# Expert weights loaded as pairs of units, 128 rows of 8 KB, into six buffers, on a one-core Trainium2 decoder step

## The chip, the cores and the metric

The kernel is one program on one core of a Trainium2 chip. The metric is the device time of one execution in microseconds (us); the time of a kernel is the median over its runs. The profile is of one execution, and its span is counted from the first to the last instruction.

## The reference

The reference is one inference step of a 2-layer decoder for 264 tokens (256 of a prompt and 8 samples), d_model = 1024, all in float32. What the change touches is the expert layer at the end of layer 1:

```python
def _swiglu(h, wg, wu, wd):
    return (jax.nn.silu(h @ wg) * (h @ wu)) @ wd

def _moe(h, router, wg, wu, wd):
    logits = jnp.einsum('btd,de->bte', h.astype(jnp.float32), router.astype(jnp.float32))
    top_v, top_i = lax.top_k(logits, TOP_K)            # TOP_K = 2 of N_EXPERTS = 8
    probs = jax.nn.softmax(top_v, axis=-1)
    gates = jnp.sum(jax.nn.one_hot(top_i, N_EXPERTS, dtype=jnp.float32) * probs[..., None], axis=-2)
    y = jnp.zeros_like(h)
    for e in range(N_EXPERTS):                          # wg, wu: 1024 x 2816, wd: 2816 x 1024
        y = y + gates[..., e:e + 1].astype(h.dtype) * _swiglu(h, wg[e], wu[e], wd[e])
    return y
```

## The kernel before, in words

The program has four stages in a row: the mixer of layer 0, its dense FFN, the mixer of layer 1, and the experts. Each engine has its own instruction stream, and semaphores are all that orders one against another.

**Jobs and units.** The tokens that chose an expert are gathered in jobs of at most 96 rows (CAP). Each job is one pass of a loop (`Fori(0, n_jobs)`) on PE, ACT, DVE and SP, and reads all weights of its expert. The weights are cut on the host in 66 units (N_FFN) of 128 partitions x 4 KB, 512 KB each: units 0 to 43 hold gate and up columns (11 chunks of 256 columns, four units a chunk: gate with the first and the second half of the 1024 input features, then up with both), and units 44 to 65 hold 128 rows each of the down matrix. In DRAM the units of all experts lie behind one another, so a unit is 512 contiguous KB.

**The path of a unit.** SP loads it into one of 11 slots (RING_X): six of the tensor `ring`, four in `early`, one in `qkv`. ACT copies it, rounded to fp32r, to one of four buffers `w_hi` (L773). DVE subtracts that from the unit and writes the rest to `w_lo` (L1233), which bumps `lo_done`. PE then multiplies with it (L1286, function `split_products`: hi x hi, hi x lo, lo x hi), 12 matmuls of 256 columns in a gate or up unit and 6 of 512 columns in a down unit. ACT takes a `w_hi` buffer again once PE has used the unit four back.

**What SP waits for.** SP issues in order. In `load_units` (L429) the load of a unit waits until the low part of the unit that was last in its slot, 11 units back, is done. It doesn't wait for PE. After unit 43 of each job SP issues `load_rows`: the token rows of the next job (384 KB, L435) and 0.8 KB of gates and token numbers (L437).

**Around the chunks.** When the products of a chunk are complete, ACT makes silu of the gate part (L783), DVE multiplies it by the up part into `prod_job` (L1251), PE turns that in two transposes of 96 rows x 128 columns (L1632), ACT and DVE split the turned part (L788, L1255). These are the stationary side of the down products. Around unit 52 PE turns the next job's token rows (L1576) and ACT and DVE split them. In units 3 to 6 the output of the job before is spread to the tokens with 16 matmuls (L1586, L1587).

**Before job 0.** The normalized rows of the second layer are turned to token-major form: PE transposes (L1548), and ACT copies three groups of 128 x 1024 from PSUM to `h_tok` (L743; the profile calls it by its tensor, `gs`). From there POOL scatters the rows to `h_rows` in DRAM (L493), and PE gathers the rows of job 0 (L1566) when DVE has worked out the routing (the last of it `take`, L1184). The first six units are loaded as the slots come free in the mixer (L406), five more once the state outputs are stored (L422).

Of the kernel before, what the change touches and what calls it, by code (L numbers as in the profile page):

```python
# [24 lines left out]
ALU = mybir.AluOpType  # L25
ACT = mybir.ActivationFunctionType
# [4 lines left out]
P = 128  # L31
D = 1024
# [23 lines left out]
N_FFN = 66  # L56
N_LAYER = N_PROJ + N_MIX + N_WO
RING = 6
SPLIT = 4
LEAD = 3  # L60
CHUNK = 256
# [7 lines left out]
NEXT_H = 52  # L69
RING_X = 11  # L70
Y_AT = 3
# [7 lines left out]
def build(nc, a, o):  # L79

    ctx = ExitStack()
    with ctx:
# [3 lines left out]
        def sem(name):  # L86
            return ctx.enter_context(nc.semaphore(name))
# [135 lines left out]

        slot_loaded = [sem(f"slot_loaded{i}") for i in range(RING_X)]
        units_used = sem("units_used")
# [140 lines left out]
        def uses_before(position):  # L366

            return sum(1 for p in ordinal if p < position and p % RING == position % RING)


        n0 = [uses_before(first_position("experts") + s) for s in range(RING)] + [0] * (RING_X - RING)

        def slot_x(s):

            if s < RING:
                return ring[:, s, :, :].rearrange("p k n -> p (k n)")
            if s < RING + 4:
                return early[:, (s - RING) * D:(s - RING + 1) * D]
            return qkv[:, :, :].rearrange("p t n -> p (t n)")[:, 0:D]

# [15 lines left out]
        def _(sp):  # L396
# [18 lines left out]
            for i in range(N_LAYER):  # L415
                load_static("mix1", i, a["w_mixer"][1, PROJ[i] if i < N_PROJ else i])
            for i in range(RING):
                load_static("experts", i, a["w_exp"][i])
            sp.wait_ge(state_out, 16 * 4 * DEPTH)
            sp.wait_ge(units_used, base_ord["mix1"] + N_PROJ + N_MIX)  # L420
            for i in range(RING, RING_X):
                sp.dma_start(slot_x(i), a["w_exp"][i]).then_inc(slot_loaded[i], 16)  # L422

            def load_units(expert, job, r0, r1):
                with sp.Fori(r0, r1) as r:
                    for s in range(RING_X):

                        sp.wait_ge(lo_done, job * N_FFN + r * RING_X + (n_split + s + 1 - RING_X))
                        sp.dma_start(slot_x(s), a["w_exp"][bass.ds(expert * N_FFN + r * RING_X + s, 1), :, :].rearrange("a p n -> p (a n)")  # L429
                                     ).then_inc(slot_loaded[s], 16)  # L430

# [6 lines left out]

            late = N_FFN // RING_X * 2 // 3
            load_units(0, 0, 1, late)  # L440
            sp.wait_ge(rows_stored, 16 * 12)
            load_rows(0)
            load_units(0, 0, late, N_FFN // RING_X)
            sp.wait_ge(jobs_done, 1)
            n_jobs = sp.value_load(jobs[0:1, MAX_JOBS:MAX_JOBS + 1], min_val=2, max_val=MAX_JOBS)
            with sp.Fori(1, n_jobs) as job:
                expert = sp.value_load(jobs[0:1, bass.ds(job, 1)], min_val=0, max_val=NE - 1)
                load_units(expert, job, 0, late)
                load_rows(job)
                load_units(expert, job, late, N_FFN // RING_X)  # L450

# [54 lines left out]
        def _(act):  # L506
# [38 lines left out]
            for l in range(DEPTH):  # L545
# [193 lines left out]
                else:  # L739

                    for m in range(3):
                        act.wait_ge(h_tr, m + 1)
                        A(h_tok[:, m, :], psum[:, (0, 2, 6)[m]:(0, 2, 6)[m] + 2, :].rearrange("p b n -> p (b n)"), ACT.Copy).then_inc(h_tok_done, 1)  # L743
                    act.wait_ge(gates_exp_in, 1)
# [17 lines left out]
                    with act.Fori(0, n_jobs) as job:  # L762
                        for u in range(N_FFN):

                            if u == Y_AT:

                                y_high(job)
                            act.wait_ge(slot_loaded[u % RING_X], job * (16 * N_FFN // RING_X) + 16 * (n0[u % RING_X] + u // RING_X + 1))
                            if buffer_x(u) == Y_AT % SPLIT and u < Y_AT + SPLIT:
                                act.wait_ge(scatter_mm, job * KD + KD)  # L770
                            else:
                                act.wait_ge(units_used, job * N_FFN + (base_ord["experts"] + used_before_x(u) + 1))
                            A(w_hi[:, buffer_x(u), :], slot_x(u % RING_X), ACT.Copy).then_inc(hi_done, 1)  # L773
                            if u == NEXT_H + 1:
# [23 lines left out]
        def _(dve):  # L798
# [50 lines left out]
            for l in range(DEPTH):  # L849
# [278 lines left out]
                else:  # L1128
# [101 lines left out]
                    with dve.Fori(0, n_jobs) as job:  # L1230
                        for u in range(N_FFN):
                            dve.wait_ge(hi_done, job * N_FFN + (n_split + u + 1))
                            V.tensor_tensor(w_lo[:, buffer_x(u), :], slot_x(u % RING_X), w_hi[:, buffer_x(u), :], ALU.subtract).then_inc(lo_done, 1)  # L1233
                            if u == Y_AT - 1:
# [32 lines left out]
        def _(pe):  # L1267
# [40 lines left out]
            for l in range(DEPTH):  # L1308
# [228 lines left out]
                else:  # L1537
# [56 lines left out]
                    with pe.Fori(0, n_jobs) as job:  # L1594
                        for u in range(N_FFN):
# [28 lines left out]
                            if u % 4 == 3 and 0 <= ch < NCH:  # L1624

                                pe.wait_ge(chunk_done, job * NCH + (ch + 1))
                                if ch >= 2:
                                    pe.wait_ge(act_lo_done, job * NCH + (ch - 1))
                                elif ch == 0:
                                    pe.wait_ge(down_taken, job * KD + 2 * KD)  # L1630
                                for i in range(2):
                                    last = nc.tensor.transpose(psum[:, 4 + ch % 2, i * CAP:(i + 1) * CAP], prod_job[:, ch % 2, i * P:(i + 1) * P], ident[0:CAP, 0:CAP])  # L1632
                                last.then_inc(act_tr, 1)
# [132 lines left out]
```

## Time and profile before

| | |
|---|---|
| median of 3 runs | 1713.52 us (1711.02 to 1717.63) |
| the profiled execution | 1717.27 us, span 1715.5 us |
| expert stage | from about 872 us of the span to its end, 8 jobs |
| loads of the queue q1 | 103888 packets, 375.15 MB |
| mean granted TensorE clock | 0.965 |

In the rows below, a busy time is that of an engine in us, PE is the matrix engine, PEld its weight loads, DVE the vector engine, ACT the scalar engine, SPq the DMA queue's issuing engine. The durations of matmuls overlap, as the engine is pipelined; their pace is read from their starts.

### The profile page before, as it was taken

What the parts mean: (1) busy time and instruction counts of PE and PEld (TensorE: products, weight loads), DVE (VectorE), ACT (ScalarE), POOL (GpSimd) and SP (SyncE); (2) the same over time, 40 slices, a digit from 0 to 9 for tenths busy, and PEclk for the clock granted to TensorE, in tenths of its full rate; (3) what the DMA queues carried; (4) which work ended last, traced back from release to release, by engine and by line L of the source; (5) the groups of instructions that cost most, each with busy time, mean ns of one, the idle gap of its engine ahead of it and who ended that gap; (6) DMA issues with size and microseconds to landing.
All of it is one profiled execution on the core that took longest, in us unless ns stands there. A gap on an engine that the chain in (4) does not pass through costs nothing.

```text
span 1715.5 us, 30826 instructions
## 1 busy us (share of the span) xinstructions
PE 1596.8 (93%) x10899; PEld 1436.0 (84%) x10899; DVE 1215.6 (71%) x1740; ACT 941.4 (55%) x1299; POOL 34.5 (2%) x53
## 2 busy tenths in 40 slices
PE   6998999899998998999879999999999999999995
PEld 4988977899986988977779797897979889797984
DVE  4777755544203776855369898898989889898984
ACT  4632242444103642242258787777877778787773
POOL 0000002000000000000030000000000000000000
PEclk9999799999999999899789999999999999999997
DMA  6542135855444541124369999998998999899990
GB/s 250 183 92 62 38 92 176 304 180 181 129 149 153 200 116 50 50 88 164 135 215 362 352 335 348 339 372 302 370 352 330 347 341 368 310 359 356 331 353 32
DMA packets 108453, 397.39 MB, mean 232 GB/s; under 512 B 13553, under 2 KB 13600, under 8 KB 107616
## 3 DMA queue, kind: packets, MB, share of 16 engines
q1 hardware_dynamic: 103888, 375.15, 61.8%
q0 software_dynamic: 4496, 21.28, 3.5%
q8 instruction: 48, 0.79, 0.2%
q14 instruction: 21, 0.17, 0.0%
HBM read 380.94 MB, written 16.43 MB: 232 GB/s over the span
## 4 chain that ended last, share of the span: by engine, by line
PE 83%; DVE 10%; ACT 4%; issue 2%; DMA 1%; SPq 0%; DVEq 0%; ACTq 0%; POOL 0%
PE psum L1286 57%; PE psum L1532 5%; PE psum L1319 3%; PE psum L1497 2%; PE psum L1499 2%; DVE w_lo L815 1%; PE psum L1392 1%; PE psum L1456 1%; PE psum L1399 1%; DVE w_lo L1233 1%; DVE qkv L885 1%; ACT w_hi L773 1%; PE psum L1403 1%; ACT w_hi L536 1%; DVE c L916 1%
## 5 line engine op out<-in xcount | busy, mean ns | idle before, releaser
L1286 PE MATMUL psum<-w_hi,h_hi 128*96 128x256 f32 x1408 | 402.0, 286 | 22.5 <-DVE w_lo L1233 22.5
L1286 PE MATMUL psum<-w_hi,h_lo 128*96 128x256 f32 x1408 | 395.2, 281 | 0.0
L1286 PE MATMUL psum<-w_lo,h_hi 128*96 128x256 f32 x1408 | 394.5, 280 | 0.0
L1233 DVE TENSOR_TENSOR w_lo<-ring,w_hi 128x1024 fp32r<-128x1024 f32 x288 | 343.3, 1221 | 33.8 <-ACT w_hi L773 33.7
L773 ACT ACTIVATE w_hi<-ring 128x1024 fp32r<-128x1024 f32 x288 | 301.9, 1058 | 28.1 <-PE psum L1286 16.9
L1286 PE MATMUL psum<-hid_hi,w_hi 128*128 128x264 f32 x992 | 290.2, 293 | 8.1 <-DVE hid_lo L821 6.1
L1286 PE MATMUL psum<-hid_lo,w_hi 128*128 128x264 f32 x992 | 285.3, 288 | 0.0
L1286 PE MATMUL psum<-hid_hi,w_lo 128*128 128x264 f32 x992 | 285.0, 287 | 0.0
L1233 DVE TENSOR_TENSOR w_lo<-early,w_hi 128x1024 fp32r<-128x1024 f32 x192 | 231.0, 1222 | 36.0 <-ACT w_hi L773 36.0
L1286 PEld LDWEIGHTS psum<-w_hi,h_hi 128*96 128x96 f32 x1408 | 228.8, 162 | 27.1 <-DVE w_lo L1233 26.4
L1286 PEld LDWEIGHTS psum<-w_hi,h_lo 128*96 128x96 f32 x1408 | 229.0, 163 | 0.0
L1286 PEld LDWEIGHTS psum<-w_lo,h_hi 128*96 128x96 f32 x1408 | 228.4, 162 | 0.3
L773 ACT ACTIVATE w_hi<-early 128x1024 fp32r<-128x1024 f32 x192 | 201.4, 1057 | 41.1 <-PE psum L1587 19.6
L815 DVE TENSOR_TENSOR w_lo<-ring,w_hi 128x1024 fp32r<-128x1024 f32 x124 | 150.4, 1220 | 81.4 <-ACT w_hi L536 81.3
L536 ACT ACTIVATE w_hi<-ring 128x1024 fp32r<-128x1024 f32 x124 | 130.7, 1058 | 136.3 <-PE psum L1286 94.7
L1286 PEld LDWEIGHTS psum<-hid_hi,w_hi 128*128 128x128 f32 x992 | 191.0, 193 | 12.9 <-issue 8.1
L1286 PEld LDWEIGHTS psum<-hid_lo,w_hi 128*128 128x128 f32 x992 | 191.4, 193 | 0.1
L1286 PEld LDWEIGHTS psum<-hid_hi,w_lo 128*128 128x128 f32 x992 | 190.3, 192 | 0.0
L1286 PE MATMUL psum<-w_hi,hid_hi 128*96 128x512 f32 x352 | 140.6, 399 | 11.5 <-DVE w_lo L1233 11.5
L1286 PE MATMUL psum<-w_hi,hid_lo 128*96 128x512 f32 x352 | 138.3, 393 | 0.0
L1286 PE MATMUL psum<-w_lo,hid_hi 128*96 128x512 f32 x352 | 137.9, 392 | 0.0
L916 DVE SCALAR_TENSOR_TENSOR c<-u_pad,prm,c 128x256 f32<-128x256 f32 x240 | 97.0, 477 | 0.0
(301 smaller groups left out, 1962.1 us busy)
## 6 DMA issues: line engine op xcount, KB each, us to landing
ring<-in_w_exp SPq DMA_DIRECT2D x288, 512.0 KB, 5.4
early<-in_w_exp SPq DMA_DIRECT2D x192, 512.0 KB, 5.4
ring<-in_w_mixer SPq DMA_DIRECT2D x112, 512.0 KB, 3.5
ring<-in_w_ffn SPq DMA_DIRECT2D x66, 512.0 KB, 3.5
qkv<-in_w_exp SPq DMA_DIRECT2D x48, 512.0 KB, 5.6
h_rows<-work POOLq DMA_DIRECT2D x12, 480.0 KB, 14.1
early<-in_s POOLq DMA_DIRECT2D x2, 2048.0 KB, 8.5
out_ss<-early POOLq DMA_DIRECT2D x2, 2048.0 KB, 9.1
```

Of the source, the lines that this page charges most:

```text
L536: A(w_hi[:, n % SPLIT, :], ring[:, p % RING, :, :].rearrange("p k n -> p (k n)"), ACT.Copy).then_inc(hi_done, 1)
L773: A(w_hi[:, buffer_x(u), :], slot_x(u % RING_X), ACT.Copy).then_inc(hi_done, 1)
L815: V.tensor_tensor(w_lo[:, n % SPLIT, :], ring[:, p % RING, :, :].rearrange("p k n -> p (k n)"), w_hi[:, n % SPLIT, :], ALU.subtract).then_ ...
L885: ins = V.scalar_tensor_tensor(qkv[:, t, 0:TP], q_pad[:, t, tap:tap + TP], w, qkv[:, t, 0:TP], ALU.mult, ALU.add)
L916: ins = V.scalar_tensor_tensor(c[:, j, 0:TP], u_pad[:, j, tap:tap + TP], w, c[:, j, 0:TP], ALU.mult, ALU.add)
L1233: V.tensor_tensor(w_lo[:, buffer_x(u), :], slot_x(u % RING_X), w_hi[:, buffer_x(u), :], ALU.subtract).then_inc(lo_done, 1)
L1286: last = M(out, lhs[x], rhs[w], start=(start and n == 0), stop=(stop and n == 2))
L1319: last = M(psum[:, i % 4, 0:T], w[:, k, :], hT[:, k, :], start=(k == 0), stop=(k == KD - 1))
L1392: last = M(pair(4)[:, u, :], units(7)[:, u, :], units(4)[:, u, :], start=True, stop=True)
L1497: M(psum[:, 2 * (t % 2), 0:T], w[:, j, :], c[:, j, :], start=(j == 0), stop=(j == CT - 1))
L1499: last = M(psum[:, 2 * (t % 2) + 1, 0:T], w[:, CT + h, :], qkv[:, 8 + h, :], start=(h == 0), stop=(h == H - 1))
L1532: last = M(psum[:, 6 + t % 2, 0:T], w[:, i % KD, :], act_all[:, f, :], start=(f == 0), stop=(f == FT - 1))
```

## The change

The same DRAM array is read as pairs: the 256 rows of two neighbouring units are taken two by two, so that partition p (of 128) gets rows 2p and 2p+1 of the pair, 8 contiguous KB. The first half of what a partition gets is "unit" 2g for the engines, the second half "unit" 2g+1. A unit now holds the even or the odd rows of the pair, so the other side of the products is put in the same order: `h_tok` is written by six copies of 128 x 512 whose innermost step is 512 elements, in place of three of 128 x 1024, and the transposes of `prod_job` read every second column. The host lays out nothing differently.

The 11 slots of 4 KB become six of 8 KB (three in `ring`, two in `early`, one in `qkv`). `SLOT_OF` gives the slot of each of the 33 pairs of a job: slots 0 to 5 three times over, then 0 to 4 three times over. A load waits until both units of the pair that was last in its slot have their low parts, six pairs back for pairs 5 to 22 and five back for the others, over the end of a job too. ACT waits for the load at each first unit of a pair. SP's loop over rounds of 11 units is written out as 33 loads.

```diff
--- before.py
+++ after.py
@@ -67,7 +67,8 @@
 JOB_ROWS = (MAX_JOBS + 1) * CAP
 ZERO_ROWS = 120
 NEXT_H = 52
-RING_X = 11
+PAIRS = N_FFN // 2
+SLOT_OF = list(range(6)) * 3 + list(range(5)) * 3
 Y_AT = 3
 
 
@@ -221,7 +222,8 @@
         jobs = ctx.enter_context(nc.sbuf_tensor("jobs", [P, MAX_JOBS + 1], mybir.dt.int32))
 
 
-        slot_loaded = [sem(f"slot_loaded{i}") for i in range(RING_X)]
+        slot_loaded = [sem(f"slot_loaded{i}") for i in range(RING)]
+        pair_loaded = [sem(f"pair_loaded{i}") for i in range(6)]
         units_used = sem("units_used")
         x_loaded = sem("x_loaded")
         consts_loaded = sem("consts_loaded")
@@ -368,15 +370,30 @@
             return sum(1 for p in ordinal if p < position and p % RING == position % RING)
 
 
-        n0 = [uses_before(first_position("experts") + s) for s in range(RING)] + [0] * (RING_X - RING)
-
-        def slot_x(s):
-
-            if s < RING:
-                return ring[:, s, :, :].rearrange("p k n -> p (k n)")
-            if s < RING + 4:
-                return early[:, (s - RING) * D:(s - RING + 1) * D]
-            return qkv[:, :, :].rearrange("p t n -> p (t n)")[:, 0:D]
+        per_job = [SLOT_OF.count(i) for i in range(6)]
+        w_pairs = a["w_exp"].rearrange("(g a) (q r) n -> g (a q) (r n)", a=2, r=2)
+
+        def pair_slot(i):
+
+            if i < 3:
+                return ring[:, 2 * i:2 * i + 2, :, :].rearrange("p s k n -> p (s k n)")
+            if i < 5:
+                return early[:, (i - 3) * 2 * D:(i - 2) * 2 * D]
+            return qkv[:, :, :].rearrange("p t n -> p (t n)")[:, 0:2 * D]
+
+        def slot_x(u):
+
+            return pair_slot(SLOT_OF[u // 2])[:, u % 2 * D:(u % 2 + 1) * D]
+
+        def loads_before(p):
+
+            return SLOT_OF[:p].count(SLOT_OF[p])
+
+        def pair_before(p):
+
+            for back in range(1, PAIRS):
+                if SLOT_OF[p - back] == SLOT_OF[p]:
+                    return p - back
 
         def buffer_x(u):
 
@@ -414,20 +431,25 @@
                 load_static("ffn", i, a["w_ffn"][i])
             for i in range(N_LAYER):
                 load_static("mix1", i, a["w_mixer"][1, PROJ[i] if i < N_PROJ else i])
-            for i in range(RING):
-                load_static("experts", i, a["w_exp"][i])
+            for i in range(3):
+                for p in (first_position("experts") + 2 * i, first_position("experts") + 2 * i + 1):
+                    before = max(q for q in ordinal if q < p and q % RING == p % RING)
+                    if before in split_ord:
+                        sp.wait_ge(lo_done, split_ord[before] + 1)
+                    else:
+                        sp.wait_ge(units_used, ordinal[before] + 1)
+                sp.dma_start(pair_slot(i), w_pairs[i]).then_inc(pair_loaded[i], 16)
             sp.wait_ge(state_out, 16 * 4 * DEPTH)
             sp.wait_ge(units_used, base_ord["mix1"] + N_PROJ + N_MIX)
-            for i in range(RING, RING_X):
-                sp.dma_start(slot_x(i), a["w_exp"][i]).then_inc(slot_loaded[i], 16)
-
-            def load_units(expert, job, r0, r1):
-                with sp.Fori(r0, r1) as r:
-                    for s in range(RING_X):
-
-                        sp.wait_ge(lo_done, job * N_FFN + r * RING_X + (n_split + s + 1 - RING_X))
-                        sp.dma_start(slot_x(s), a["w_exp"][bass.ds(expert * N_FFN + r * RING_X + s, 1), :, :].rearrange("a p n -> p (a n)")
-                                     ).then_inc(slot_loaded[s], 16)
+            for i in range(3, 6):
+                sp.dma_start(pair_slot(i), w_pairs[i]).then_inc(pair_loaded[i], 16)
+
+            def load_pairs(expert, job, p0, p1):
+                for p in range(p0, p1):
+
+                    sp.wait_ge(lo_done, job * N_FFN + (n_split + 2 * pair_before(p) + 2))
+                    sp.dma_start(pair_slot(SLOT_OF[p]), w_pairs[bass.ds(expert * PAIRS + p, 1), :, :].rearrange("g p n -> p (g n)")
+                                 ).then_inc(pair_loaded[SLOT_OF[p]], 16)
 
             def load_rows(job):
 
@@ -436,18 +458,18 @@
                 sp.wait_ge(y_lo_done, job + 1)
                 sp.dma_start(meta_job[0:CAP, :], meta_rows[bass.ds(job * CAP, CAP), :]).then_inc(meta_loaded, 16)
 
-            late = N_FFN // RING_X * 2 // 3
-            load_units(0, 0, 1, late)
+            late = 22
+            load_pairs(0, 0, 6, late)
             sp.wait_ge(rows_stored, 16 * 12)
             load_rows(0)
-            load_units(0, 0, late, N_FFN // RING_X)
+            load_pairs(0, 0, late, PAIRS)
             sp.wait_ge(jobs_done, 1)
             n_jobs = sp.value_load(jobs[0:1, MAX_JOBS:MAX_JOBS + 1], min_val=2, max_val=MAX_JOBS)
             with sp.Fori(1, n_jobs) as job:
                 expert = sp.value_load(jobs[0:1, bass.ds(job, 1)], min_val=0, max_val=NE - 1)
-                load_units(expert, job, 0, late)
+                load_pairs(expert, job, 0, late)
                 load_rows(job)
-                load_units(expert, job, late, N_FFN // RING_X)
+                load_pairs(expert, job, late, PAIRS)
 
 
         @block.gpsimd
@@ -740,7 +762,10 @@
 
                     for m in range(3):
                         act.wait_ge(h_tr, m + 1)
-                        A(h_tok[:, m, :], psum[:, (0, 2, 6)[m]:(0, 2, 6)[m] + 2, :].rearrange("p b n -> p (b n)"), ACT.Copy).then_inc(h_tok_done, 1)
+                        for b in range(2):
+                            ins = A(h_tok[:, m, :].rearrange("p (r k b q) -> p b k q r", r=2, k=4, b=2)[:, b],
+                                    psum[:, (0, 2, 6)[m] + b, :].rearrange("p (k q r) -> p k q r", k=4, r=2), ACT.Copy)
+                        ins.then_inc(h_tok_done, 1)
                     act.wait_ge(gates_exp_in, 1)
                     A(rt[:, 3, 0:3], rt[:, 2, 0:3], ACT.Exp).then_inc(gates_exp, 1)
 
@@ -765,12 +790,13 @@
                             if u == Y_AT:
 
                                 y_high(job)
-                            act.wait_ge(slot_loaded[u % RING_X], job * (16 * N_FFN // RING_X) + 16 * (n0[u % RING_X] + u // RING_X + 1))
+                            if u % 2 == 0:
+                                act.wait_ge(pair_loaded[SLOT_OF[u // 2]], job * (16 * per_job[SLOT_OF[u // 2]]) + 16 * (loads_before(u // 2) + 1))
                             if buffer_x(u) == Y_AT % SPLIT and u < Y_AT + SPLIT:
                                 act.wait_ge(scatter_mm, job * KD + KD)
                             else:
                                 act.wait_ge(units_used, job * N_FFN + (base_ord["experts"] + used_before_x(u) + 1))
-                            A(w_hi[:, buffer_x(u), :], slot_x(u % RING_X), ACT.Copy).then_inc(hi_done, 1)
+                            A(w_hi[:, buffer_x(u), :], slot_x(u), ACT.Copy).then_inc(hi_done, 1)
                             if u == NEXT_H + 1:
                                 gathered(job + 1, 0)
                                 gathered(job + 1, 1)
@@ -1230,7 +1256,7 @@
                     with dve.Fori(0, n_jobs) as job:
                         for u in range(N_FFN):
                             dve.wait_ge(hi_done, job * N_FFN + (n_split + u + 1))
-                            V.tensor_tensor(w_lo[:, buffer_x(u), :], slot_x(u % RING_X), w_hi[:, buffer_x(u), :], ALU.subtract).then_inc(lo_done, 1)
+                            V.tensor_tensor(w_lo[:, buffer_x(u), :], slot_x(u), w_hi[:, buffer_x(u), :], ALU.subtract).then_inc(lo_done, 1)
                             if u == Y_AT - 1:
                                 y_low(job)
                             if u == Y_AT + 1:
@@ -1629,7 +1655,7 @@
                                 elif ch == 0:
                                     pe.wait_ge(down_taken, job * KD + 2 * KD)
                                 for i in range(2):
-                                    last = nc.tensor.transpose(psum[:, 4 + ch % 2, i * CAP:(i + 1) * CAP], prod_job[:, ch % 2, i * P:(i + 1) * P], ident[0:CAP, 0:CAP])
+                                    last = nc.tensor.transpose(psum[:, 4 + ch % 2, i * CAP:(i + 1) * CAP], prod_job[:, ch % 2, i:CHUNK:2], ident[0:CAP, 0:CAP])
                                 last.then_inc(act_tr, 1)
                             if u == NEXT_H:
                                 turn_rows(job)
```

## Rows read from the trace of the kernel before

**Rows 1.** The page: busy time and chain.

```profile
PE 1596.8 (93%) x10899; PEld 1436.0 (84%) x10899; DVE 1215.6 (71%) x1740; ACT 941.4 (55%) x1299; POOL 34.5 (2%) x53
...
PE 83%; DVE 10%; ACT 4%; issue 2%; DMA 1%; SPq 0%; DVEq 0%; ACTq 0%; POOL 0%
```

**Rows 2.** PE, PEld, DVE, ACT, POOL busy; granted clock, DMA share, GB/s.

```profile
800.00:900.00 100.00, 81.30 (x551) 78.17 (x550) 53.94 (x124) 38.46 (x50) 14.57 (x13) 0.85 0.52 189
...
1000.00:1100.00 100.00, 96.41 (x695) 86.38 (x694) 87.91 (x100) 77.64 (x92) 0.00 (x0) 1.00 0.94 345
```

**Rows 3.** Chain that ended last, over one job: start, length.

```profile
993.04 5.66 PE psum L1286 x48
998.69 0.17 PE psum L1632 x2
998.86 5.65 PE psum L1286 x48
...
1045.42 5.54 PE psum L1286 x24
...
1059.18 1.07 ACT w_hi L773
1060.27 1.24 DVE w_lo L1233
...
1094.51 5.54 PE psum L1286 x47
```

**Rows 4.** Waits in 1051 to 1153 us: total, times, longest.

```profile
DVE w_lo L1233 <- ACT w_hi L773: 9.6, 30, 1.6
...
PE psum L1286 <- DVE w_lo L1233: 3.6, 3, 1.4
...
ACT w_hi L773 <- PE psum L1587: 2.4, 1, 2.4
```

**Rows 5.** Waits of SP's queue, 800 to 1600 us.

```profile
SPq L429 <- DVE w_lo L1233: 459.3, 435, 47.3
```

**Rows 6.** Windows inside the job that begins at 977 us.

```profile
1010.00:1025.00 15.00, 15.00 (x131) 15.00 (x130) 13.76 (x18) 11.84 (x17) 0.00 (x0) 1.00 0.99 346
1025.00:1040.00 15.00, 15.00 (x131) 15.00 (x130) 13.76 (x15) 12.23 (x17) 0.00 (x0) 1.00 1.01 362
1040.00:1055.00 15.00, 15.00 (x91) 12.13 (x90) 13.55 (x16) 12.23 (x14) 0.00 (x0) 1.00 1.02 409
```

**Rows 7.** DMA issues of the whole run: KB, median us to landing.

```profile
ring<-in_w_exp SPq DMA_DIRECT2D x288, 512.0 KB, 5.4
...
xT<-in_xT SPq DMA_DIRECT2D x1, 1056.0 KB, 5.0
```

**Rows 8.** DMA issues between 1028 and 1040 us.

```profile
ring<-in_w_exp SPq DMA_DIRECT2D x6, 512.0 KB, 7.1
```

**Rows 9.** Line L429: landing, shortest, median, longest.

```profile
DMA to landing us min/median/max: 3.1/5.4/8.9
```

**Rows 10.** DVE, 1050 to 1100 us: start, length.

```profile
1061.41 6.90 DVE L1233 TENSOR_TENSOR w_lo<-ring,w_hi 128x1024 fp32r<-128x1024 f32 x6
```

**Rows 11.** ACT, 1040 to 1100 us: start, length.

```profile
1071.53 1.06 ACT L773 ACTIVATE w_hi<-early 128x1024 fp32r<-128x1024 f32 x1 [0.33 <-PE psum L1286]
```

**Rows 12.** Packets of the first 12 us.

```profile
DMA packets 955, 3.97 MB, mean 330 GB/s; under 512 B 112, under 2 KB 112, under 8 KB 827
```

**Rows 13.** Groups by form, from 700 us.

```profile
L1632 PE MATMUL psum<-consts,work 96*128 96x96 f32 x176 | 29.0, 245 | 0.0
...
L1632 PEld LDWEIGHTS psum<-consts,work 96*128 96x128 f32 x176 | 23.0, 141 | 1.3
...
L743 ACT ACTIVATE gs<-psum 128x1024 f32<-128x1024 f32 x3 | 3.1, 1023 | 18.9 <-PE psum L1548 18.9
```

**Rows 14.** ACT before job 0: start, length.

```profile
853.13 1.02 ACT L743 ACTIVATE gs<-psum 128x1024 f32<-128x1024 f32 x1 [0.68 <-PE psum L1548]
```

**Rows 15.** PE before job 0: start, length.

```profile
860.08 8.69 PE L1566 MATMUL psum<-work,gs 128*128 128x96 f32 x48 [5.08 <-DVE work L1184]
```

## The prediction

> **What bounds the kernel now.** I read the page first: PE is busy 93% of the span and holds 83% of the chain that ended last, DMA 1% of it [rows 1]. So a transfer can only matter where it hides badly, and the next question is where in the 1715.5 us that could be. The windows by stretch answer it: in the expert stage PE is busy 96.41 of 100 us at a granted clock of 1.00 (the 2.4 GHz level), DVE 87.91, ACT 77.64, while the DMA engines show a share of 0.94 and 345 GB/s [rows 2]. That share looks like a second bound, and the case turns on whether it is one.
>
> The chain inside a job shows the pace. A group of four gate and up units is 48 matmuls in 5.65 us plus two transposes in 0.17 us; from 993.04 to 998.86 us is 5.82 us [rows 3]. From 993.04 to 1094.51 us, the same place one job on, is 101.47 us [rows 3]; eight such jobs are 812 us. The waits of a job name no DMA at all: PE waits 3.6 us for `w_lo`, behind the turn of the token rows and the spreading of the output; DVE waits 9.6 us for ACT and ACT 2.4 us for PE at its longest named row [rows 4]. SP's queue on the other hand waits 459.3 us for `w_lo` [rows 5]: the loads are held back by slots, not the engines by loads.
>
> Last, the windows within a job. Between 1010 and 1055 us the DMA share is 0.99 to 1.02 all along while the rate goes from 346 to 409 GB/s, and PE is busy 15.00 of 15 us in each of the three [rows 6]. So the rate of the queue changes by 18% and PE doesn't notice. The slots absorb it.
>
> **The change, part by part**, against the profiled execution's 1717.27 us (3.75 us above the median of 1713.52).
>
> *Larger transfers.* 528 loads of 512 KB become 264 of 1 MB. They are not on the chain; their price is a landing time that has to fit in the slots. The nearest row for one alone is `xT`, 1056 KB, landed after 5.0 us [rows 7]; its rows of 8448 bytes are the 128 packets above 8 KB among the first 955 (955 less 827) [rows 12], so a row of 8 KB should be one packet as well. Under load I add to a landing of 512 KB the time that the second 512 KB takes at 409 GB/s [rows 6], 1.3 us: 5.4 + 1.3 = 6.7 us at the median [rows 7], 7.1 + 1.3 = 8.4 us where the token rows are in the queue [rows 8], 8.9 + 1.3 = 10.2 us for the longest [rows 9].
>
> *Slots.* What a slot allows is the time between its uses. With six pairs in turn that is 12 units at 5.82 / 4 us = 17.5 us; with five, from pair 23 to pair 4 of the next job, 10 units. The fastest of these are down units, 5.54 us for 24 matmuls, four units, so 1.385 us each [rows 3], 13.85 us for ten. A slot is held from the start of ACT's first copy to the end of the second subtraction: one unit, then 1.07 and 1.24 us [rows 3], together 3.7 to 3.8 us. With 8.4 us of landing that makes 12.2 of 13.85 us, with 5.0 us 8.8; the margin is 1.6 to 5 us. Before, a slot had 11 units, 16.0 us, and used 7.1 + 2.3. So the margin shrinks but stays. The tightest place, directly: pair 32 (units 64 and 65) takes the slot of units 54 and 55. Unit 55 is the first of the six subtractions that begin at 1061.41 and take 6.90 us, so it ends at 1062.6 [rows 10]; ACT begins unit 64 at 1071.53 [rows 11]. That leaves 8.9 us for a landing of 5.0 to 8.4 us, and behind ACT there is more: it copies up to three units ahead of PE. Cost 0.
>
> *SP's queue.* Behind a waiting load stand the following loads and `load_rows`; pair 21 takes the place of unit 43 before it, and waits for unit 31 where unit 43 waited for unit 32, so the token rows leave about a unit (1.45 us) earlier. Half of the DMA issues go away, on an engine that mostly waits. In the mixer's end three pairs wait for two free slots each; these loads and three more are first used at job 0, so at most a unit's time goes, and nobody waits. Cost 0.
>
> *ACT's waits.* 33 fewer in each job. ACT is idle 22 of 100 us [rows 2]; 0.
>
> *Copies to `h_tok`.* Three of 1023 ns become six of half the size [rows 13]. If only the elements cost, 0.5 us more for fixed parts; if each write with its step of 2 KB took twice as long, three pairs of about 2.0 us. The last copy starts at 853.13 and is over at 854.15 [rows 14]; PE begins the gather at 860.08, after waiting for DVE's `take` [rows 15]. The cover is 5.9 us, and 0.5 to 3.1 us more disappears in it. Cost 0; without the cover it would be those 3.1 us once.
>
> The Trainium skill ("SBUF — State Buffer", the note on cachelines) has SBUF lines of 16 bytes and full speed while two accesses hit one line. By that, the 2 KB step of these copies pays, and the 8-byte step of the transposes, next, is free; taking the one or the other leaves the sum as it is, because of the cover in rows 14 and 15.
>
> *Transposes.* 176 in the run, 22 in a job, in the chain at 0.17 us a pair [rows 3]. Their weights, 96 x 128, are now read with a step of two elements. No such weight load is in the trace of before. From below: 0, if a load takes the 141 ns of today [rows 13] and hides as today. From above: each takes 141 ns longer and none hides, 176 x 0.141 = 24.8 us. I take 0: the load must become twice as long before anything shows, the chain's 0.17 us for two transposes and two loads leaves no room for two bare loads of 141 ns, so they overlap something today [rows 3, 13], and half a doubling, 12.4 us, I keep for the range.
>
> The sum is 0 against 1717.27, and as the profiled execution stands 0.2% above the median, I put the forecast at the median: 1713.5 us. 0.5% is 8.6 us, about what a measurement of this kernel can tell from no change.
>
> **Rivals.**
>
> *A. The fifth slot is missed (slower).* In the stretch with five slots a pair that lands after more than 13.85 - 3.8 = 10.05 us holds up ACT, then PE. For it: a margin of 1.6 us at the loaded median, and a longest landing that would come to 10.2. Against it: that longest one stands where six slots are in use, and in the down stretch the rate is 409 GB/s. If a pair lands after twice the median of a unit, 10.8 us, each round loses 0.75 us: three rounds in each of eight jobs, 18 us, 1731.5 us.
>
> *B. Strided weight loads (slower).* As above, 12.4 us for half of the doubling, 24.8 for all: 1726 to 1738 us. For it: PE has no slack, all of it would show. Against it: the loads are short beside a down matmul's 5.54 / 24 = 0.23 us, and the pair of transposes is already two loads close together.
>
> *C. The queue is the bound after all (faster).* A share of 1.01 [rows 6] would be read as saturation. Were it so, the gate and up stretch, 64 us of a job, would go at 409 in place of 362 GB/s, 11% of 64 is 7.4 us, eight times 59 us: 1654 us. Against it stands the PE column of the same rows.
>
> The Trainium skill ("DMA: Bandwidth & Descriptors", the section on bandwidth) asks for 1 MiB or more in a transfer to get three quarters of the peak; here transfers of half that already ran at 409 GB/s [rows 6]. By that rule the change would pay only if C held.
>
> *D. The 8 KB rows are cut to 4 KB packets again.* The change is then only coarser waiting; the time is that of the forecast.
>
> **How the numbers follow.** No change within 0.5%, D included: 0.79. A 0.05, B 0.06, other things that slow it (a wait in the routing) 0.02: slower 0.13. C 0.03, and 0.05 for a gain from some wait that the waits view doesn't name: faster 0.08. The likeliest case alone would lie within 1708 to 1721, the spread of single runs. The range reaches into A's price and B's half, and by the same amount less to the other side: 1704 to 1730.
>
> **What the profile after would show.** Queue q1 with 103888 - 33792 - 4224 = 65872 packets (half of the 528 x 128 of data, and 16 short ones fewer for each of 264 loads; the 112 short packets of the first stretch are seven times sixteen [rows 12]); below about 70000 it says that D is wrong. Landings of 6.5 to 8.5 us. The period of a job 101.5 us, 0.17 us for a pair of transposes; 0.3 or more, and L1632's loads above 141 ns, is B. No DMA among what ACT waits for at L773; any there, above all at units 46 to 65, is A. PE's 48 matmuls below 5.65 us would be C. L743 x6 of 0.6 us each, more if the step costs, with the gather still behind DVE. The prediction is wrong if the period moves by more than 1 us.

## The result: 0.25% slower, and the profile after

The changed kernel takes 1718.23 us (median of 20 runs, 1714.67 to 1721.16) against 1713.49 us (20 runs, 1711.02 to 1717.74). The ratio is 1.0025 with a 95% interval of 1.0016 to 1.0034. The loss is smaller than the half per cent within which the prediction spoke of no change, but the interval is clear of zero, so there is a loss where none was forecast. The profiled execution's span grew from 1715.5 to 1718.8 us. Two executions further down stand far above the others of their kernels, 2305.96 us in experiment 3 and 3185.81 us in experiment 9 (PE at half its rate in all stages), and the ratios leave them out.

The page of the changed kernel, its span, busy times, the queue q1 and the chain:

```profile
span 1718.8 us, 29480 instructions
...
PE 1600.6 (93%) x10899; PEld 1439.9 (84%) x10899; DVE 1215.5 (71%) x1740; ACT 944.1 (55%) x1302; POOL 34.2 (2%) x53
...
q1 hardware_dynamic: 65872, 375.14, 60.1%
...
PE 83%; DVE 10%; ACT 4%; issue 2%; DMA 1%; SPq 0%; DVEq 0%; ACTq 0%; POOL 0%
```

PE holds the same 83% of the chain [rows 1] and is 3.8 us busier. Queue q1 has the 65872 packets that the prediction worked out, so each row of 8 KB went as one packet; its share is 60.1% where it was 61.8%, by the page of before:

```profile
q1 hardware_dynamic: 103888, 375.15, 61.8%
```

The chain in the same job as in [rows 3] (start, length; L1658 is the transposes of before's L1632, L1312 is before's L1286):

```profile
993.15 0.20 PE psum L1658 x2
993.35 5.66 PE psum L1312 x48
999.00 0.20 PE psum L1658 x2
999.21 5.66 PE psum L1312 x48
...
1046.09 5.55 PE psum L1312 x24
...
1095.03 0.20 PE psum L1658 x2
1095.23 4.83 PE psum L1312 x41
```

The 48 matmuls of a group of four units take 5.66 us, where they took 5.65 or 5.66, and the pair of transposes takes 0.20 where it took 0.17 us: 5.86 us from 993.35 to 999.21, where it was 5.82. From 993.35 to 1095.23 is 101.88 us, the job before was 101.47. Eight times 0.41 us is 3.3 us, the whole difference of the two spans.

The groups by form that answer to [rows 13] (busy us, then the mean of one in ns):

```profile
L1658 PE MATMUL psum<-consts,work 96*128 96x96 f32 x176 | 32.0, 263 | 0.0
...
L1658 PEld LDWEIGHTS psum<-consts,work 96*128 96x128 f32 x176 | 28.5, 195 | 0.8
...
L766 ACT ACTIVATE gs<-psum 128x512 f32<-128x512 f32 x6 | 5.5, 1092 | 17.6 <-PE psum L1574 17.6
```

A weight load of the transposes takes 195 ns where it took 141. The copies to `h_tok` are six, 1092 ns each, for half of what one copy of 1023 ns did.

The loads (KB, median us to landing), against [rows 7]:

```profile
ring<-in_w_exp SPq DMA_DIRECT2D x144, 1024.0 KB, 4.9
early<-in_w_exp SPq DMA_DIRECT2D x96, 1024.0 KB, 4.9
```

and the windows that answer to [rows 6]:

```profile
1010.00:1025.00 15.00, 15.00 (x131) 15.00 (x130) 13.65 (x16) 12.06 (x16) 0.00 (x0) 1.00 0.95 365
1025.00:1040.00 15.00, 15.00 (x131) 15.00 (x130) 13.67 (x17) 12.03 (x16) 0.00 (x0) 1.00 0.84 312
1040.00:1055.00 15.00, 15.00 (x94) 12.38 (x93) 13.44 (x16) 11.89 (x15) 0.00 (x0) 1.00 0.97 371
```

At the median a load of 1 MB lands after 4.9 us, sooner than one of 512 KB did (5.4 us). The DMA share in these windows is 0.95, 0.84 and 0.97 where it was about 1; from 900 to 1600 us it is 0.90 where it was 0.93. PE is busy 15.00 of 15 us in all three windows, as before, so nobody makes use of the relief.

### The profile page after: what moved, and what is told of

The parts are those of the page before. It is cut to its first block, busy times and chain, and to the rows that moved or that the text cites. A ratio compares the mean times of both kernels' runs of the same rounds, so it can differ in the third digit from the quotient of the medians.

```text
span 1718.8 us, 29480 instructions
## 1 busy us (share of the span) xinstructions
PE 1600.6 (93%) x10899; PEld 1439.9 (84%) x10899; DVE 1215.5 (71%) x1740; ACT 944.1 (55%) x1302; POOL 34.2 (2%) x53
## 3 DMA queue, kind: packets, MB, share of 16 engines
q1 hardware_dynamic: 65872, 375.14, 60.1%
## 4 chain that ended last, share of the span: by engine, by line
PE 83%; DVE 10%; ACT 4%; issue 2%; DMA 1%; SPq 0%; DVEq 0%; ACTq 0%; POOL 0%
PE psum L1312 57%; PE psum L1558 5%; PE psum L1345 3%; PE psum L1523 2%; PE psum L1525 2%; DVE w_lo L841 1%; PE psum L1418 1%; PE psum L1482 1%; PE psum L1425 1%; DVE w_lo L1259 1%; DVE qkv L911 1%; ACT w_hi L799 1%; PE psum L1429 1%; PE psum L1658 1%; ACT w_hi L558 1%
## 5 line engine op out<-in xcount | busy, mean ns | idle before, releaser
L1312 PE MATMUL psum<-w_hi,h_hi 128*96 128x256 f32 x1408 | 402.1, 286 | 22.2 <-DVE w_lo L1259 22.2
L1312 PE MATMUL psum<-w_hi,h_lo 128*96 128x256 f32 x1408 | 395.7, 281 | 0.0
L1312 PE MATMUL psum<-w_lo,h_hi 128*96 128x256 f32 x1408 | 394.0, 280 | 0.0
L1312 PE MATMUL psum<-hid_hi,w_hi 128*128 128x264 f32 x992 | 290.0, 292 | 8.1 <-DVE hid_lo L847 6.1
L1312 PE MATMUL psum<-hid_lo,w_hi 128*128 128x264 f32 x992 | 285.3, 288 | 0.0
L1312 PE MATMUL psum<-hid_hi,w_lo 128*128 128x264 f32 x992 | 284.9, 287 | 0.0
L1312 PEld LDWEIGHTS psum<-w_hi,h_hi 128*96 128x96 f32 x1408 | 231.4, 164 | 26.8 <-DVE w_lo L1259 26.1
L1312 PEld LDWEIGHTS psum<-w_hi,h_lo 128*96 128x96 f32 x1408 | 229.1, 163 | 0.0
L1312 PEld LDWEIGHTS psum<-w_lo,h_hi 128*96 128x96 f32 x1408 | 228.4, 162 | 0.3
L1312 PEld LDWEIGHTS psum<-hid_hi,w_hi 128*128 128x128 f32 x992 | 190.9, 192 | 12.8 <-issue 8.1
L1312 PEld LDWEIGHTS psum<-hid_lo,w_hi 128*128 128x128 f32 x992 | 191.4, 193 | 0.1
L1312 PEld LDWEIGHTS psum<-hid_hi,w_lo 128*128 128x128 f32 x992 | 190.3, 192 | 0.0
L1312 PE MATMUL psum<-w_hi,hid_hi 128*96 128x512 f32 x352 | 140.5, 399 | 11.5 <-DVE w_lo L1259 11.5
L1312 PE MATMUL psum<-w_hi,hid_lo 128*96 128x512 f32 x352 | 138.5, 393 | 0.0
L1312 PE MATMUL psum<-w_lo,hid_hi 128*96 128x512 f32 x352 | 137.8, 392 | 0.0
```

The lines of the kernel that those rows point to most:

```text
L1312: last = M(out, lhs[x], rhs[w], start=(start and n == 0), stop=(stop and n == 2))
```

## The experiments

All times are against the kernel before on the same chip.

**1. The pairs without the stepped transposes.** In the changed kernel:

```diff
-transpose(..., prod_job[:, ch % 2, i:CHUNK:2], ...)
+transpose(..., prod_job[:, ch % 2, i * P:(i + 1) * P], ...)
```

> The pairs, the six slots and the new copies to h_tok stay; only the transposes of prod_job read neighbouring columns again. So the down products meet the wrong rows of the weights, and the outputs are not the reference's; sizes and counts of the work are the same. Theory T (the weight loads with a step of two elements cost it: 141 to 196 ns each, a pair of transposes 0.17 to 0.20 us in the chain): period of a job back to 101.5 us, span 3.3 us below the changed kernel's 1718.8, time within 0.1% of before. Rival L (the coarser loads cost it, through later landings or other packets): the time stays 3 to 5 us above before and a pair of transposes is at 0.17 us all the same. Rival H (the copies to h_tok delay the start of the jobs): also stays above before, with job 0 starting later.

Measured: 1715.11 against 1714.86 us, ratio 1.0001 (0.9991 to 1.0010). Its chain, the first group of two jobs that follow each other, and its weight loads by form:

```profile
991.46 5.66 PE psum L1312 x48
...
1092.93 5.66 PE psum L1312 x48
```

```profile
L1658 PEld LDWEIGHTS psum<-consts,work 96*128 96x128 f32 x176 | 23.0, 141 | 1.3
```

From 991.46 to 1092.93 is 101.47 us, the job of before to a hundredth, and the load is back at 141 ns. Loads of 1 MB in six slots, with the waits that go with them, neither cost nor bring anything that can be measured.

**2. The kernel before with the stepped transposes alone.** The same edit the other way round, in the kernel before.

> The kernel before, with one edit: the transposes of prod_job read every second column. The down products meet the wrong rows, so the outputs are not the reference's. Theory T: L1632's weight loads go from 141 to 196 ns, a pair of transposes from 0.17 to 0.20 us, a job from 101.47 to 101.9 us, the span from 1715.5 to 1718.8 us, the time 0.2% above before. Rivals L and H: no difference to before.

Measured: 1717.57 us, ratio 1.0021 (1.0012 to 1.0031). Chain and weight loads:

```profile
988.84 0.20 PE psum L1632 x2
989.04 5.66 PE psum L1286 x48
...
1090.92 5.66 PE psum L1286 x48
```

```profile
L1632 PEld LDWEIGHTS psum<-consts,work 96*128 96x128 f32 x176 | 28.5, 195 | 0.8
```

From 989.04 to 1090.92 is 101.88 us. This one edit has the price of the whole change: 0.21% here, 0.25% for the change, each interval holding the other's value. The span of this profile, 1713.2 us, lies below before's 1715.5 and says nothing of the edit: the mean granted clock of that execution is 0.970 where before's was 0.965, and the difference lies ahead of the experts, above all in the first 300 us (0.97, 0.99 and 0.96 by 100 us, where before had 0.95, 0.95 and 0.93). The period of a job, at a granted clock of 1.00, is the measure for an effect of 3 us.

**3. The kernel before with the stepped copies to `h_tok` alone.**

```diff
-A(h_tok[:, m, :], psum[:, b0:b0 + 2, :], ACT.Copy)          # b0 = (0, 2, 6)[m]
+for b in range(2):
+    A(h_tok[:, m, :].rearrange("p (r k b q) -> p b k q r", r=2, k=4, b=2)[:, b],
+      psum[:, b0 + b, :].rearrange("p (k q r) -> p k q r", k=4, r=2), ACT.Copy)
```

> The kernel before, with one edit: the three copies to h_tok become the six with a step of 512 elements, so the experts get their features in an order that does not fit the weights and the outputs are not the reference's. Theory T: the six copies take 5.5 us in place of 3.1, end by 855.2 us of the span and hide behind the routing, the gather starts at 860 us as before; time within 0.1% of before. Rival H: the gather or the first copy to w_hi begins later, and the time goes up by 1 us or more.

Measured: 1713.07 us, ratio 0.9994 (0.9984 to 1.0004). ACT and PE before job 0 (start, length):

```profile
846.68 5.55 ACT L744 ACTIVATE gs<-psum 128x512 f32<-128x512 f32 x6 [17.57 <-PE psum L1551]
```

```profile
855.97 8.14 PE L1569 MATMUL psum<-work,gs 128*128 128x96 f32 x48 [5.08 <-DVE work L1187]
```

The copies end at 852.23, PE begins the gather at 855.97, still released by DVE's `take`: 3.7 us of cover are left. (This execution began the copies at 846.68 us where before began them at 849.72, 3.0 us earlier, and the gather 4.1 us earlier.) No price.

**4. The changed kernel with the order made by DVE.**

```diff
-V.tensor_tensor(prod_job[:, ch % 2, :], silu_job[:, ch % 2, :], psum[0:CAP, 2 + ch % 2, 0:CHUNK], ALU.mult)
+V.tensor_tensor(prod_job[:, ch % 2, :].rearrange("p (i q) -> p q i", i=2),
+                silu_job[:, ch % 2, :].rearrange("p (q i) -> p q i", i=2),
+                psum[0:CAP, 2 + ch % 2, 0:CHUNK].rearrange("p (q i) -> p q i", i=2), ALU.mult)
```

with the transposes of experiment 1.

> The changed kernel, and the reference's outputs: DVE writes prod_job already sorted into even and odd columns (both its inputs read and its output written in runs with a step), and the transposes read neighbouring columns. Theory T: the weight loads are back at 141 ns and 0.17 us a pair; DVE's 410 ns for the product may grow, by up to twice, 0.4 us four units apart on an engine that is idle 12 of 100 us, so the time is within 0.1% of before, 3 to 4 us below the changed kernel. If DVE's product stood on the path, or grew to over 1 us, the time would go up by some 0.1 us for each of 88 chunks or more. Rival L: stays 3 to 5 us above before.

Measured: 1715.26 us, ratio 1.0000 (0.9992 to 1.0009). Groups by form, first the product in the kernel before, then this run, and this run's chain:

```profile
L1251 DVE TENSOR_TENSOR work<-work,psum 96x256 f32<-96x256 f32 x88 | 36.0, 409 | 0.0
```

```profile
L1277 DVE TENSOR_TENSOR work<-work,psum 96x256 f32<-96x256 f32 x88 | 54.8, 622 | 0.0
...
L1660 PEld LDWEIGHTS psum<-consts,work 96*128 96x128 f32 x176 | 23.0, 141 | 1.3
```

```profile
989.83 5.66 PE psum L1314 x48
...
1091.42 5.65 PE psum L1314 x48
```

The expectation has the inputs read with a step too, which they are not: both are read in the order of before, and only the writes are out of order, each some 128 elements from the one before it. DVE pays 622 where it paid 409 ns for the product, 11 times in a job, on an engine with 12 of 100 us to spare, and PE's loads are at 141 ns. A job takes 101.59 us, 0.12 above before; eight times that is 1 us, which lies inside the interval. So this form has the pairs at a price that the timed runs can't tell from none. It is faster than the changed kernel (the two intervals don't meet) and no faster than the kernel before.

**5 and 6. A longer step.** DVE writes `prod_job` spread out, and the transposes read with a step of four or eight elements in place of two (`prod_job` gets two or four times the room, for eight in another part of `work`):

```diff
-V.tensor_tensor(prod_job[:, ch % 2, :], ...)
+V.tensor_tensor(prod_job[:, ch % 2, 0:2 * CHUNK:2], ...)                # 0:4 * CHUNK:4 in the other
-transpose(..., prod_job[:, ch % 2, i:CHUNK:2], ...)
+transpose(..., prod_job[:, ch % 2, 2 * i:2 * CHUNK:4], ...)             # 4 * i:4 * CHUNK:8
```

> The changed kernel, and the reference's outputs: DVE writes prod_job into every second element of rows twice as long, so the transposes read with a step of four elements (16 bytes) where the changed kernel has two. Theory T, in the form that the price grows with the distance between elements: a weight load above 196 ns (some 300 ns if it goes on by 55 ns for each element of step), a pair of transposes near 0.35 us in the chain, 10 us or more above the changed kernel. Rival F (any step costs the same once, as the load leaves a fast form that needs neighbouring elements): 196 ns and 0.20 us again, the time as the changed kernel's, 0.2 to 0.3% above before.

> As the run with a step of four, with prod_job in another part of the tensor work, DVE writing every fourth element and the transposes reading with a step of eight (32 bytes). The outputs are the reference's. By growth with distance: above the step of four again. By rival F: 196 ns and 0.20 us as with two. A third way: the price stops growing where each element lies in a line of its own; then four and eight are equal, and above two.

Measured: 1716.81 us, 1.0016 (1.0008 to 1.0025) with four; 1717.69 us, 1.0020 (1.0008 to 1.0031) with eight. Groups by form, first four, then eight:

```profile
L1277 DVE TENSOR_TENSOR work<-work,psum 96x256 f32<-96x256 f32 x88 | 36.2, 411 | 0.0
...
L1658 PEld LDWEIGHTS psum<-consts,work 96*128 96x128 f32 x176 | 28.8, 199 | 0.8
```

```profile
L1277 DVE TENSOR_TENSOR work<-work,psum 96x256 f32<-96x256 f32 x88 | 54.0, 613 | 0.0
...
L1658 PEld LDWEIGHTS psum<-consts,work 96*128 96x128 f32 x176 | 27.6, 188 | 0.9
```

Loads of 199 and 188 ns beside 195 with two, a pair of transposes at 0.20 and 0.19 us in the chain, and 101.97 and 101.90 us for a job: the price does not grow with the distance, from two to eight elements. My expectation of growth fell, and so did the third way (four and eight above two); of rival F's words the runs bear out that one price holds for all three steps, not why. DVE's writes behave otherwise: every second element costs nothing (411 ns), every fourth does (613 ns), as did the step of 128 of experiment 4 (622 ns).

**7 and 8. Fewer slots.** In the changed kernel:

```diff
-SLOT_OF = list(range(6)) * 3 + list(range(5)) * 3
+SLOT_OF = list(range(5)) * 5 + list(range(4)) * 2                       # five slots
+SLOT_OF = list(range(4)) * 6 + list(range(3)) * 3                       # four slots
```

> The changed kernel with five slots of 8 KB in place of six, five pairs back and four over the end of a job (pairs 29 to 32 and 0 to 4). The outputs are the reference's. By the sum of the prediction a slot with four in turn has 8 x 1.385 = 11.1 us in the down units, and holds 3.8 us of work beside a landing of 4.9 us (the changed kernel's median): 8.7, margin 2.4. So theory M (the slots have a margin, the prediction's rival A was far): no change to the changed kernel, ACT waits for no DMA. Rival A (the margin was nearly used up with six): 5 us or more above the changed kernel, with DMA among what ACT waits for.

> The changed kernel with four slots, three in turn for pairs 27 to 32 and 0 to 2. The outputs are the reference's. By the same sum: 6 x 1.385 = 8.3 us where 8.7 are needed, so here the wait must come: theory M expects 0.4 us or more for each of three rounds in eight jobs, 10 to 40 us above the changed kernel, with DMA named before ACT's copies in the down units. If nothing happens, the sum of the prediction counts something twice, and the slots have more room than it says.

Measured: five slots 1716.77 us, 1.0022 (1.0011 to 1.0032), the price of the changed kernel and no more, with no DMA in any wait of ACT after 860 us. But its loads are the same and land later:

```profile
ring<-in_w_exp SPq DMA_DIRECT2D x168, 1024.0 KB, 6.0
early<-in_w_exp SPq DMA_DIRECT2D x96, 1024.0 KB, 5.9
```

So the sum with five slots is 5.9 + 3.8 = 9.7 of 11.1 us, a margin of 1.4 and not of 2.4 us.

Four slots 1733.31 us, 1.0123 (1.0098 to 1.0147). The chain with four slots over a job, with the down units inside it, and ACT's waits between 1000 and 1100 us (total, times, longest):

```profile
992.27 5.66 PE psum L1312 x48
...
1062.44 4.83 DMA ring<-in_w_exp
...
1067.37 1.07 ACT w_hi L799
...
1069.61 1.23 DVE w_lo L1259
...
1071.02 4.81 DMA ring<-in_w_exp
...
1075.92 0.13 ACT L799
1076.04 1.17 issue
1077.21 1.07 ACT w_hi L799
...
1095.91 4.12 PE psum L1312 x35
```

```profile
ACT w_hi L799 <- DMA ring<-in_w_exp: 5.5, 6, 2.1
...
ACT L799 <- DMA ring<-in_w_exp: 0.9, 1, 0.9
ACT w_hi L799 <- DMA early<-in_w_exp: 0.2, 1, 0.2
```

Here is rival A as it looks when it comes: the chain goes from a landing of 4.83 us to the copy that waited for it, to DVE's subtraction, and from there to the next load. One round, 1062.44 to 1071.02, is 8.58 us. The prediction's sum for a slot, with the landing that the changed kernel has, gives 4.9 + 3.8 = 8.7 us, and three pairs of down units last 8.3 us: so the sum finds the edge, between three and four pairs in turn. The changed kernel never has fewer than five.

The sum finds where the loss begins, not how large it is. A job from 992.27 to 1095.91 takes 103.64 us, 1.7 more than the changed kernel's 101.9 (other jobs up to 3.4 more), where three rounds of 0.4 us make 1.2. One part of the rest is ACT's table load, 0.13 + 1.17 us from 1075.92, which here stands in the chain behind a landing and in the changed kernel's chain does not. In the timed runs four slots are 16.5 us above five, which have the changed kernel's time; 10 to 40 us were expected.

**9 and 10. The order made by the moving side.** In the changed kernel, with the transposes of experiment 1:

```diff
-[w[:, s, kk * CHUNK:(kk + 1) * CHUNK] for w in (w_hi, w_lo)]
+[w[:, s, kk * CHUNK:(kk + 1) * CHUNK].rearrange("p (q i) -> p i q", i=2) for w in (w_hi, w_lo)]
```

> The changed kernel, and the reference's outputs: the transposes read neighbouring columns, and the sorting into even and odd columns is done by the gate and up matmuls, whose moving side (w_hi, w_lo) is read with a step of two elements, 4224 matmuls in the run. If a step costs only on the side of the weight loads: matmuls at 0.118 us apart as before, 48 in 5.65 us, a pair of transposes 0.17 us, the time as before's. If the moving side pays as well, by the 55 ns for 128 columns that the weight loads showed, it would be 110 ns for 256 columns, the pace would near double, and the time rise by some 465 us; by any lower price in proportion.

> The kernel of the stepped moving side once more, for a profile at the pace of its timed runs (2154 us): the profiled execution of that run took 3186 us, with PE at half its rate in all stages, the mixer's too, and shows nothing of the step. Expected: the gate and up matmuls some 0.22 us apart (0.118 us plus 441 us over 4224 matmuls, 0.104 us), 48 of them in 10.7 us, the down units and all before the experts as in the changed kernel. If the 441 us were elsewhere, the 48 would stay at 5.65 us.

Measured: 2154.45 us, ratio 1.2571 (1.2541 to 1.2601), and 2158.09 us for the one execution of the second run, against 1716.84 us. The profile is that of the second run. Its chain:

```profile
895.56 0.17 PE psum L1658 x2
895.72 10.89 PE psum L1312 x48
...
906.78 10.94 PE psum L1312 x48
...
995.63 5.55 PE psum L1312 x24
```

48 matmuls take 10.89 us in the first group of a job and 10.94 in the others, in place of 5.66, so 0.110 us more for each matmul of 256 columns. The 24 matmuls of 512 neighbouring columns take 5.55 us as ever, and a pair of transposes 0.17 us. Over 4224 matmuls 0.110 us would make 465 us; 441 came. Most of the difference can be followed: a job (the first groups begin at 895.72 and 1052.72) takes 157.0 us, 55.5 more than before and not the 58.1 of 528 matmuls, and PE's waits for `w_lo` in a job are one of 1.4 us where they were three of 3.6 us in all [rows 4]. That is 2.2 us of the 2.6 of each job, and eight jobs make 21 of the 24 us. The same step that costs 3 us on 176 weight loads costs 441 us on the moving side.

## Why the prediction was wrong

The range held the time (1718.2 in 1704 to 1730). The forecast of no difference did not: there is a loss of 0.25%, and the runs show one cause.

*The step that failed: transposes.* The prediction bounded them by 0 and 24.8 us and took 0, because "the load must become twice as long before anything shows". That was argued from the chain's 0.17 us for a pair, from which I read that two loads of 141 ns overlap something. Experiments 1 and 2 show it wrong in both directions: the load grew by 54 ns, well short of twice, and 0.037 us of the 0.11 us that a pair has gained is in the chain at once (0.41 us over 11 pairs). 88 pairs at 0.037 us are 3.3 us, 0.19%; the intervals of change and experiment 2 hold that. Rival B was the mechanism, at 13% of its full price. The prediction gave it 0.06, because it priced only a doubling that shows in full or half of it; a load on a pair of instructions that already sits bare in the chain had to be expected to show in part. That the pair is in the chain stood in [rows 3]; the size of 54 ns stood in no row of before. Why a step makes the load longer, and why by the same for every step tried, stays open.

The Trainium skill ("SBUF — State Buffer", the note on cachelines) would have the 8-byte step of the transposes free. The measurement decides against it for float32 weights on PE: 141 ns without a step, 195, 199 and 188 ns with steps of 8, 16 and 32 bytes, and on the moving side 0.110 us for 256 columns at 8 bytes. DVE's writes do go by it: nothing at 8 bytes (411 ns), more at 16 (613 ns).

*Larger transfers.* Hidden, as said; the landing was overestimated, 6.7 us at the median against 4.9. The prediction took it as a property of the size, and it is not: in the changed kernel and the four others with the same six slots and packets (experiments 1, 4, 5 and 6) the median of the line is 4.9 to 5.2 us, with five slots 5.9 us. It moves with the number of slots (by when the loads leave, I take it; that is not shown). The queue's share does not: 59.7 to 60.5% in all these and with four slots, 61.8 to 62.0% wherever loads are of 512 KB (before, experiments 2 and 3). So the lower share goes with the larger loads, and the early landing needs the six slots as well.

*Slots.* Right: no wait for a load, and experiments 7 and 8 put the edge where the sum puts it. Rival A needed another slot gone, and then one more. (Of pair 5 the text above says that it waits for the pair six back. It waits for the one 21 back, the last in its slot, and as SP issues in order it leaves right behind pair 4, at 974.80 us for the job shown. No sum uses it.)

*Copies to `h_tok`.* 5.54 us in place of 3.1, 2.4 more, within the 0.5 to 3.1 that were allowed, and hidden behind DVE's routing. In the changed kernel:

```profile
849.66 5.54 ACT L766 ACTIVATE gs<-psum 128x512 f32<-128x512 f32 x6 [17.56 <-PE psum L1574]
```

```profile
860.06 8.71 PE L1592 MATMUL psum<-work,gs 128*128 128x96 f32 x48 [5.08 <-DVE work L1210]
```

They end at 855.20 where they ended at 854.15 [rows 14], and PE starts at 860.06, where it started at 860.08 [rows 15]. Here the Trainium skill's note, by which a step of 2 KB pays, agrees with the trace: 1092 ns for 512 elements against 1023 for 1024 (no run has a copy of 512 elements without the step).

*SP's queue and ACT's waits.* Nothing that can be measured, as said; experiment 1 holds both and is at 1.0001.

*Rival C.* Refuted by the change itself: the DMA share fell and PE's pace stayed at 5.66 us for 48 matmuls. Rival D is refuted by the packet count.

*Where the gain of the larger loads went.* There was none to be had: PE sets the pace of the expert stage and waits for no transfer. What the change earned, half the DMA issues for the expert weights and a lower share of the queue, stays as slack.

## What to carry to other kernels

When a layout change moves a permutation to the other operand, price it at each place that it could be done, and keep it off PE when PE is the bound: here a sorting of this kind cost 2.4 us on ACT that hid behind other work, 0.12 us a job on DVE (inside the noise of the timed runs), 3.3 us in all on PE's weight loads and 441 us on its moving side. A cost that is bounded between 0 and something, on instructions that the chain names, is not 0. And a busy share of the DMA queues near 1 is no bound while the slots' holding time (landing, copy, subtraction) is below the time until they are needed again; that sum gave 8.7 us for a round that took 8.58, with a landing measured in a neighbouring kernel. The landing itself has to be measured for each number of slots (4.9 us with six, 5.9 with five).

## What was unexpected of the hardware

PE's weight loads of 96 x 128 float32 pay the same for each step tried (195, 199, 188 ns for 2, 4, 8 elements, against 141), while DVE's writes pay nothing for a step of two (411 against 410 ns) and half as much again for four (613 ns). The duration of a weight load is not its own alone: the one without a step took 141 ns behind matmuls of the usual pace and 159 ns in experiment 10, behind the slow ones. So the price of a step is read between kernels with the same neighbours. And loads of 1 MB in rows of 8 KB landed after 4.9 us with six slots and after 5.9 us with five, in a stream in which loads of 512 KB in rows of 4 KB, in eleven slots, landed after 5.4.
